# Two matmuls for three in the 256 column parts of both MLP products, with the halves added by VectorE

## The reference, cut to what matters

```python
h = rms_norm(x, g_mix) * (1.0 + scale1) + shift1
...                                   # Fourier mixing, gated recurrence, W_out
x = x + gate1 * mix
h = rms_norm(x, g_mlp) * (1.0 + scale2) + shift2
ff = jnp.square(jax.nn.relu(h @ w_ff1)) @ w_ff2
return x + gate2 * ff                 # then a final RMSNorm
```

## Time and profile before

| | |
|---|---|
| runs | 1405.68 to 1405.81 us, median 1405.74 |
| profiled execution, first to last instruction | 1403.9 us |
| PE busy | 1382.1 us (98%), 7652 matmuls |
| DVE, ACT, POOL busy | 803.1 (57%), 588.1 (42%), 477.7 us (34%) |
| mean granted TensorE clock | 0.999 of full speed |
| bytes over HBM | 231 MB, 164 GB/s over the span |

### The profile page before, as it was taken

One profiled execution on the slowest core, in us unless ns is written; L12 is line 12 of the kernel. 1 busy time (PEld: TensorE's weight loads), 2 busy tenths in 40 slices (PEclk: granted clock), 3 DMA queues, 4 the chain that ended last, 5 costly groups with the idle time before them and its releaser, 6 DMA issues.

```text
span 1403.9 us, 18642 instructions
## 1 busy us (share of the span) xinstructions
PE 1382.1 (98%) x7652; PEld 1188.1 (85%) x7652; DVE 803.1 (57%) x761; ACT 588.1 (42%) x703; POOL 477.7 (34%) x269
## 2 busy tenths in 40 slices
PE   5999999999999999999999999999999999999998
PEld 3877778898888888888888888888888888888887
DVE  5967688785438974554334543353645334344584
ACT  5667888565325632333222232332222223323152
POOL 0002111145003765474554545531432222333131
PEclk9999999999999999999999999999999999999999
DMA  9444411116210343334433343489997444445552
GB/s 370 167 158 157 158 61 38 46 31 222 109 60 31 120 165 128 141 134 153 144 117 121 120 157 140 162 293 389 373 381 275 151 150 155 166 171 198 201 189 90
DMA packets 75701, 231.30 MB, mean 165 GB/s; under 512 B 5729, under 2 KB 9953, under 8 KB 66786
## 3 DMA queue, kind: packets, MB, share of 16 engines
q1 hardware_dynamic: 75074, 229.60, 44.4%
q10 hardware_dynamic: 544, 0.52, 0.1%
HBM read 165.09 MB, written 65.01 MB: 164 GB/s over the span
## 4 chain that ended last, share of the span: by engine, by line
PE 95%; DVE 2%; DMA 1%; SPq 1%; issue 1%; ACT 0%; POOL 0%; DVEq 0%; ACTq 0%
PE bank L799 22%; PE bank L800 22%; PE bank L801 22%; PE bank L793 9%; PE bank L794 9%; PE bank L795 9%; DMA mod_first<-in_w_mod 1%; PE bank L828 1%; PE bank L840 0%; DVE lo_r L2152 0%; SPq L565 0%; DVE n_t L2124 0%; PE bank L810 0%; PE bank L818 0%; PE bank L849 0%
## 5 line engine op out<-in xcount | busy, mean ns | idle before, releaser
L799 PE MATMUL bank<-hin_hi,w_lo 128*128 128x512 f32 (+1 forms) x896 | 301.9, 337 | 0.0
L800 PE MATMUL bank<-hin_lo,w_hi 128*128 128x512 f32 (+1 forms) x896 | 301.4, 336 | 0.0
L801 PE MATMUL bank<-hin_hi,w_hi 128*128 128x512 f32 (+1 forms) x896 | 301.1, 336 | 0.0
L2529 POOL TENSOR_TENSOR w_lo<-w_raw,w_hi 128x2048 fp32r<-128x2048 f32 x28 | 134.7, 4812 | 321.8 <-ACT w_hi L1603 320.3
L2270 DVE TENSOR_TENSOR hin_lo<-hin,hin_hi 128x3072 fp32r<-128x3072 f32 x28 | 130.9, 4676 | 189.2 <-ACT hin_hi L1615 189.2
L799 PEld LDWEIGHTS bank<-hin_hi,w_lo 128*128 128x128 f32 x896 | 170.1, 190 | 18.1 <-issue 0.2
L800 PEld LDWEIGHTS bank<-hin_lo,w_hi 128*128 128x128 f32 x896 | 170.1, 190 | 17.6 <-issue 0.2
L801 PEld LDWEIGHTS bank<-hin_hi,w_hi 128*128 128x128 f32 x896 | 170.0, 190 | 17.8
L1603 ACT ACTIVATE w_hi<-w_raw 128x2048 fp32r<-128x2048 f32 x28 | 53.6, 1915 | 249.2 <-PE bank L801 178.4
L2521 POOL TENSOR_TENSOR w_lo<-w_raw,w_hi 128x512 fp32r<-128x512 f32 x43 | 65.3, 1519 | 183.9 <-ACT w_hi L1541 183.8
L1551 ACT ACTIVATE hid<-bank 128x768 f32<-128x768 f32 (+2 forms) x68 | 52.5, 772 | 162.8 <-PE bank L801 152.6
(11 more groups left out here) (293 smaller groups left out, 3170.5 us busy)
## 6 DMA issues: line engine op xcount, KB each, us to landing
hin<-hid_all SPq DMA_DIRECT2D x28, 1536.0 KB, 6.9
hid_all<-hid SPq DMA_DIRECT2D x105, 384.0 KB, 2.5
w_raw<-in_w_ff SPq DMA_DIRECT2D x36, 1024.0 KB, 9.2
mod_raw<-in_w_mod SPq DMA_DIRECT2D x16, 1024.0 KB, 6.5
w_raw<-in_w_ff SPq DMA_DIRECT2D x60, 256.0 KB, 3.4
x<-in_xT SPq DMA_DIRECT2D x5, 2048.0 KB, 14.5
w_sums<-w_raw SPq DMA_DIRECT2D x8, 1024.0 KB, 15.6
w_raw<-w_sums SPq DMA_DIRECT2D x8, 1024.0 KB, 9.8
```

Source lines behind the costliest of these rows:

```text
L799: pe.matmul(out, w_lo, v_hi, start=first, stop=False, skip_group_check=True)
L800: pe.matmul(out, w_hi, v_lo, start=False, stop=False, skip_group_check=True)
L801: return pe.matmul(out, w_hi, v_hi, start=False, stop=last, skip_group_check=True)
L2529: pool.tensor_tensor(w2_lo[n % 2][:].rearrange("p t n -> p (t n)"), w2_raw[m % RAWS][:].rearrange("p t n -> p (t n)"), w2_hi[n % 2][:].rea ...
```

## The change

In the 256 column parts of FF1, and of FF2 for its products j = 0 to 4 (`NSPLIT = 5`), the low and the high operand are laid so that one access pattern takes both, 2 x 256 columns. One matmul with the high weights writes both results into the two halves of a 512 column bank; a second, with the low weights, adds its 256 columns to the half of the high operand. The half of the low operand is added later by DVE: in FF1 by eight small adds a job (`add_low`) and one max-and-multiply (`relu_square`) that takes over a quarter of ACT's squared ReLU of P4; in FF2 by a second gated addition for each 256 column unit. FF2 uses eight banks in those steps instead of six. PE's products P6, P7, P4 and P2 wait for DVE's adds, and the store of P4's square waits for `relu_square`. The buffers move so that the two parts of an operand lie in one tensor; the last `w2_raw` buffer changes place with one `hin` buffer.

```diff
+A_P5, SQ_P4 = 7, 8
+ADDED = (P1, P6, P5, P2, P7, A_P5, P3, P4, SQ_P4)
+NSPLIT = 5
+SPLIT = {3: (2, 0, CH), 5: (3, 0, CH), 0: (0, 0, CH), 2: (1, 0, CH), 4: (2, CH, QC), 1: (0, CH, QC), 7: (3, CH, QC),
+         6: (1, CH, QC)}
...
+    def added(q, i):
+        return len(ADDED) * (q - 1) + ADDED.index(i) + 1
...
             else:
                 sp.wait_ge(ff1_sq, q + 1)
+                if q:
+                    sp.wait_ge(ff1_added, added(q, SQ_P4))
...
+        def three_of(out, w_hi, w_lo, v, first, last):
+            return three_more(out, w_hi, w_lo, v[:, HI], v[:, LO], first, last)
+        def three_apart(out, w_hi, w_lo, v, first, last):
+            pe.matmul(out.rearrange("p (h n) -> p h n", h=2), w_hi, v, start=first, stop=False, skip_group_check=True)
+            return pe.matmul(out[:, HI * QC:(HI + 1) * QC], w_lo, v[:, HI], start=False, stop=last,
+                             skip_group_check=True)
...
             elif i == P2:
                 after(pe, ff1_copy, 4 * q)
+                if q > 1:
+                    pe.wait_ge(ff1_added, added(q - 1, P4))
...
                 pe.wait_ge(ff1_copy, 4 * q + {P6: 1, P7: 2, P4: 3}[i])
+                if q:
+                    pe.wait_ge(ff1_added, added(q, {P6: P1, P7: P6, P4: P7}[i]))
...
-                    m = three_more(out, w1_hi[o % 4][:, w], w1_lo[o % 4][:, w], v_hi[:, kk], v_lo[:, kk],
-                                   i in (P1, P5, P2, P3) and kk == 0, kk == FT - 1)
+                    m = (three_apart if part else three_of)(
+                        out, w1_hi[o % 4][:, w], w1_lo[o % 4][:, w], pair[:, :, kk],
+                        i in (P1, P5, P2, P3) and kk == 0, kk == FT - 1)
...
+                        if j < NSPLIT and size == QC:
+                            m = three_apart(bank[k][:], w2_hi[n % 2][:, t, w], w2_lo[n % 2][:, t, w], v, first, last)
...
+        def add_low(q, i):
+            own = 2 * (q % 2)
+            buf = {P5: 1, A_P5: 1, P2: 2 - own, P3: 3}.get(i, own)
+            tile = {P1: S_B11, P2: S_B11, P7: S_B22, A_P5: S_B22, P4: S_B21}.get(i, S_T3)
+            part = hid_tile(tile, q)[:, CH:HTOK]
...
+            dve.tensor_tensor(part, ps[:, 2 * CH * buf + HTOK:2 * CH * (buf + 1)], part, ALU.add).then_inc(ff1_added, 1)
+        def relu_square(q):
+            t = hid[S_B21][:, CH:HTOK]
+            dve.wait_ge(ff1_added, added(q, P4))
+            dve.scalar_tensor_tensor(t, t, 0.0, t, ALU.max, ALU.mult).then_inc(ff1_added, 1)
...
+            if q and step in (U2, C11, C22, C12, T4):
+                dve.wait_ge(ff1_added, added(q, {U2: P5, C11: P2, C22: A_P5, C12: P3, T4: SQ_P4}[step]))
...
+            if size == QC:
+                dve.wait_ge(dve_own, mark(gated(j, dd, o, size, bank[k][:, HI * QC:(HI + 1) * QC])))
+                m = gated(j, dd, o, size, bank[k][:, LO * QC:(LO + 1) * QC])
...
         token_lo(P6, 1)
+        add_low(1, P1)
         hid_out(0, T1)
         hid_out(0, T3)
         token_lo(P2, 1)
         hid_out(0, T2)
         token_sum(3, 1)
+        add_low(1, P6)
+        add_low(1, P5)
         token_lo(P7, 1)
         token_lo(P3, 1)
         token_lo(P4, 1)
         hid_out(0, T4)
         for q in range(1, NJ):
-            for step in (U2, C11, B11):
-                hid_out(q, step)
+            for i in (P1, P6, P5):
+                if q > 1:
+                    add_low(q, i)
+            hid_out(q, U2)
+            add_low(q, P2)
+            hid_out(q, C11)
+            hid_out(q, B11)
             if q == NJ - 1:
                 hin_split_lo(0)
-            for step in (C22, B22, C12, B12, T1, T3, T2):
+            add_low(q, P7)
+            add_low(q, A_P5)
+            hid_out(q, C22)
+            hid_out(q, B22)
+            add_low(q, P3)
+            for step in (C12, B12, T1, T3, T2):
                 hid_out(q, step)
+            add_low(q, P4)
+            relu_square(q)
             if q == REST:
                 w1_add(q + 1, P7)
                 w1_add(q + 1, P3)
```

More of the change, by code:

```diff
@@ L56 @@
 NTILE = 3 * FT
+LO, HI = range(2)
 ORDER = (0, 2, 1)
@@ L312, in token_operand, with token_sums @@
-    def token_operand(i, part):
+    t1_s, t2_s, t12_s, t4_s = (place(n, [P, FT, CH], F32, o) for n, o in (
+        ("t1_s", t1_at), ("t2_s", t2_at), ("t12_s", t12_at), ("t4_s", t4_at)))
+    t1_two, t2_two, t12_two, t4_two = (place(n, [P, 2, FT, CH], F32R, o) for n, o in (
+        ("t1_two", t1_at), ("t2_two", t2_at), ("t12_two", t12_at), ("t4_two", t4_at)))
+    t4b_s = place("t4b_s", [P, FT, QC], F32, t4_at + 16384)
+    t4b_two = place("t4b_two", [P, 2, FT, QC], F32R, t4_at + 16384)
+    def token_sums(i, part):
@@ L356, in build_encoder, with hin_pair, hin_part @@
     hin_at = (A0 + 98304, A0 + 73728, A0 + 110592)
+    hin_apart = (36864, 12288, 12288)
     hin = [place(f"hin{i}", [P, GF, HTOK], F32, o) for i, o in enumerate(hin_at)]
-    hin_lo = [place(f"hin_lo{i}", [P, GF, HTOK], F32R, o) for i, o in enumerate(hin_at)]
-    hin_hi = [place(f"hin_hi{i}", [P, GF, HTOK], F32R, o) for i, o in enumerate((
-        A0 + 131072, A0 + 86016, hid_at))]
+    hin_two = [place(f"hin_two{i}", [P, 2, n // 4], F32R, o) for i, (o, n) in enumerate(zip(hin_at, hin_apart))]
+    def hin_pair(i, t, o, size):
+        return hin_two[i][:, :, t * HTOK + o:t * HTOK + o + size]
+    def hin_part(i, part):
+        return hin_two[i][:, part, 0:GF * HTOK]
     x2 = place("x2", [P, KD, T], F32, W0)
@@ L441, in build_encoder @@
     op_hi = sem("op_hi")
-    op_lo = [sem(f"op_lo{i}") for i in range(7)]
+    op_lo = sem("op_lo")
     ld_w1 = [sem(f"ld_w1_{b}") for b in range(4)]
@@ L679, in load_w2 @@
                 if m < RAWS:
-                    sp.wait_ge(ff1_mm, 7 * (NJ - 1) + (P1, P7, P7, P3, P7, P6)[m] + 1)
+                    sp.wait_ge(ff1_mm, 7 * (NJ - 1) + (P1, P7, P7, P3, P7, P4)[m] + 1)
                 else:
                     w2_freed(m - RAWS)
+                if m == RAWS - 1:
+                    for i in range(7):
+                        sp.wait_ge(st_hid[i], 16 * NJ)
                 if b < SUM1:
@@ L1154, in last_part @@
                     w = slice(dd * P, (dd + 1) * P)
-                    m = three_more(ps[:, at:at + size], w2_hi[n % 2][:, t, w], w2_lo[n % 2][:, t, w],
-                                   hin_hi[n % 3][:, t, o:o + size], hin_lo[n % 3][:, t, o:o + size],
-                                   late and n == NSTEP - 2 and t == 0, only and t == GF - 1)
+                    m = three_of(ps[:, at:at + size], w2_hi[n % 2][:, t, w], w2_lo[n % 2][:, t, w],
+                                 hin_pair(n % 3, t, o, size), late and n == NSTEP - 2 and t == 0,
+                                 only and t == GF - 1)
                 at += size
@@ L1524, in token_hi @@
                 act.wait_ge(op_sum, 4 * part + SUM_AT[part][i])
-            act.activation(v_hi, v, ACT.Copy).then_inc(op_hi, 1)
+            act.activation(token_pair(i, part)[:, HI], token_sums(i, part), ACT.Copy).then_inc(op_hi, 1)
         def split_w1_hi(q, i):
@@ L2127, in token_sum @@
         def token_sum(step, part):
-            v = {i: token_operand(i, part)[0] for i in range(7)}
+            v = {i: token_sums(i, part) for i in range(7)}
             dve.wait_ge(hhi_done, (2 * NN - 1 + part) * KD)
@@ L2399, in _ @@
             if g == GF - 1 and j < 6:
-                for u in range(NU - 1):
-                    ff2_out(j, u)
+                for u in range(units(j) - 1):
+                    (ff2_split_out if j < NSPLIT else ff2_out)(j, u)
             if n == 17:
```

172 lines of the change are left out of this document (98 added, 74 removed).

## The result

The changed kernel takes 1412.02 us in the median of four runs (1411.38 to 1413.21), the kernel before 1405.76: ratio 1.0040, 95% interval [1.0028, 1.0052]. It is slower by 6.3 us, 4.4 us above the forecast, and inside the stated range of 1400.5 to 1413. The span of the profiled execution went from 1403.9 to 1410.2 us; after the change the profiled one is the slowest of the four by 0.2 to 0.9 us.

The account below looks back on a forecast made before the run. PE was taken to bound the kernel, with 95% of the chain. Waits of 11.35 us against a gain of 9.4 us made it 2.0 us longer than 1405.74: 1407.7, written as 1407.6 us; range 1400.5 to 1413.

Parts of the forecast that it names:

- The pair: 256 column parts of FF1 and FF2: 512 plus 256 column matmul takes 347.1 ns instead of 359.4; gain 9.4 us.
- The price of an instruction itself: PE, FF1 and FF2: each matmul pays some 12.3 ns whatever its width, saved on 768 tiles.
- The places of the waits: PE waits for DVE's adds in job 1 (4.8 us with job 2), 5 with 6 (4.0), 16 and FF2's step 3.
- the cover of 10.6 us: Regular jobs of FF1: DVE idles 10.6 us before U2, so its 4 us of added work a job hides.
- Their sizes: PE's waits in FF1 and at the seam: 4.8 + 4.0 + 1.15 + 1.4 = 11.35 us.
- the rival of smaller waits: Jobs 1, 5, 16 and seam: POOL meets DVE less, waits about 6 us, time 1402.3 us; chance 0.27.
- The wait at P7 of job 5 that was to go: FF1, job 5: the existing 0.35 us wait disappears, since P7's weights are ready by then.
- Job 16 and the seam: PE waits 1.15 us before P4 of job 16 and 1.4 us at FF2's step 3, its operand late.
- The clock: A lower granted clock behind the long gaps: named as a sign of being wrong, given no price.
- POOL holding DVE more: At `relu_square` and T4 in jobs 1, 4 and 16: waits 15.1 us, time 1411.4 us; chance 0.19.
- The dearer pair: Each 512 column matmul behind a 256 starts slow: pair 355 ns, gain 3.4 us, time 1413.7 us; chance 0.09.

Follow-up runs that it names:

- one piece: Against the changed kernel: FF2's 512 column matmul reads 512 adjacent columns instead of two pieces of 256, multiplying wrong numbers; one run, 1411.35 us.
- the gap and the clock: Against the changed kernel: in job 5 DVE does the add of P1 ahead of T4 of job 4; one run, 1409.64 us.
- grouped: Against the changed kernel: 256 column parts of both products take four tiles' 512 column matmuls first, then their four 256; 1409.28 us.
- FF2's half grouped: Against the changed kernel: FF1 wholly as before the change, FF2 with all sixteen 512 column matmuls first, then the sixteen 256; 1402.52 us.
- The last of the runs above: Against the changed kernel: job 16's adds of P7 go ahead of FF2's first operand split, matmuls grouped by width in fours; one run, 1410.29 us.

## Why the prediction was nearly right, and where it was wrong

**The pair.** The step that failed is "I take 347, as both durations are the steady ones". The pair in turn cost 352.5 ns in FF2, near the dear end (355) that I had bounded and given 0.09. The reason I held against it, that the first 256 behind a 512 is short by as much, made up only a part: on the average of the step a 512 took some 8 ns more than in a row, and a 256 about 3 ns less. That it is the order of the widths is shown: 352.5, 349 and 346 ns a pair at 32, 8 and 2 changes a step, with the same matmuls, and no difference with the operand in one piece; why a 512 behind a 256 is slow stays open. My test for it, 16.46 us a step for right and 16.6 for wrong, gave 16.55. In FF1 the gain was less, 0.1 us a regular job, or 3.4 ns a tile (3.8 by the books), as the run of 512s behind such a part pays too (2.78 us for 2.75). Both products together gained 3.9 us of the 9.4. The price of an instruction itself, 12.3 ns, was right: with two changes a step it comes back whole (16.45 us). The Trainium skill, "TensorE: Matmul & The Clock Gate", section "Back-to-back issue gap", has N/2.4 plus 2.5 ns for an isolated warm matmul; the estimate from it was a gain of 1.9 us. That grouped step gave 20 x 0.21 = 4.2 us in FF2 alone, so the trace still disagrees.

**The places of the waits** were right, all of them: jobs 1, 5 with 6, 16, and step 3. None stood elsewhere, and of the regular jobs only job 6 showed one, which was forecast, as the cover of 10.6 us said (two of the others take 58.19 us, before 58.38). The row that I read those 10.6 us from is the last job's; a regular job, too, has 10.64 us of idle time there in the trace of before. That they are the adds' place in DVE's order is shown for job 5 by moving the add, for job 16 by three runs in which the adds went ahead of `hin_split_lo(0)` and the gap before P4 went, for job 2 by the wait that came there and went with one move, and for job 1 only by leaving the adds out and by the rows above.

**Their sizes** were 8.8 us for 11.35. In job 1 POOL was away: T4 of job 0 took 0.68 us and B11 1.09, not 1.78 and 1.64; that was the rival of smaller waits, true in this one place. The wait at P7 of job 5 that was to go I had priced by its idle time, 0.35 us; from start to start it cost 0.61. Job 16 and the seam came within 0.3 us; for the seam that is in part luck, for of the four profiled executions with this order of DVE in job 16 two had no wait at step 3 (one piece, and the gap and the clock) and one had 0.46 us (grouped). T4's store was due at FF1's end + 10 and its successor issued at + 9.7; of `relu_square` and T4 it was T4 that POOL held, and with DVE 3.4 us earlier it was the other.

**The clock** was not in the sum. It is 1.6 us of the miss of 4.4, the pair 5.5, the smaller waits take back 2.5, the start 0.2. I had named it as a sign of being wrong and given it no price. That it follows a gap of some 3 us in most executions is what five of them show; what decides the odd one stays open.

**Where the chances stood.** The result is above the forecast's own 1404 to 1410.5, and slower had 0.35, below the 0.4 of no change. The faster rival needed the pair and the smaller waits; the waits were smaller, the pair was not cheap. By the number, POOL holding DVE more, 1411.4 us, was nearest, but its mechanism acted at the seam alone, and there at the forecast's price: the waits were 8.8 us, not its 15.1. The dearer pair, 1413.7 us, with the least chance, had the gain nearly right, 3.4 us for 3.9. That its waits of 11.35 us come near the 10.4 of the waits and the low clock together is luck, and so is it that the forecast's misses in part cancel.

## What to carry to other kernels

Price a mixed run of instructions from rows in that mixture, or leave the first and last of a run in as the bound that weighs: two steady durations side by side left out what changing the width costs, and putting like widths together got it back. An add that PE waits for must stand ahead of work that nobody waits for in its engine's order, and where a sequence of jobs is short or starts up there may be no such place: do those jobs the old way. A wait that is taken away ahead of a join with another engine may come back behind it.

## What the runs showed of the hardware

A matmul of 512 columns behind one of 256 was followed after 0.23 to 0.24 us instead of 0.227, whether its operand lay in one piece or two.

At the seam T4, a DVE instruction with two inputs in SBUF, took 5.25 us beside a POOL instruction of 4.80, and 0.96 without. That agrees with the Trainium skill, "SBUF — State Buffer", section "Who interferes with whom", by which a DVE instruction with two SBUF inputs contends with a GpSimd instruction that reads SBUF.

The stretch at the lower clock is not bound to the long gap alone. In the profile of FF2's half grouped a stretch of 3.4 us at 1.2 GHz stands near the start, from 27.8 us on (window as above); before, the same window was at 1.00. The last of the runs above has one there too, from 27.3 us on, besides that behind its gap.

```profile
27.00:32.00 5.00, 4.31 (x19) 1.41 (x20) 3.21 (x5) 2.39 (x5) 0.00 (x0) 0.66 0.99 410
```

FF1 began 1.8 us later for it. Of the 37 runs of the kernel before that stand beside the first eight experiments, most have spans of 1403.7 to 1404.4 us at a mean clock of 0.999, and ten 1405.2 to 1405.8 at 0.998: about the same price, though without a profile of such a run its place is not known.
